# Banded attention on TensorE: query halves of 64 with their 192 keys, on quarters of the array

## The chip, the cores and the metric

The kernel runs on one core of one Trainium2 chip. The metric is the device time of one launch in microseconds, the median of three runs. All computation is in one launch; the host only lays out the inputs and outputs.

Engines are called PE (TensorE), PEld (its weight loads), DVE (VectorE), ACT (ScalarE), POOL (GpSimd) and SP (SyncE, which issues DMAs).

## The reference, cut to what matters

One step of a two-layer decoder trunk for 1024 prompt tokens and 8 sample tokens, model width 1024, fp32: a gated linear recurrence (HGRN2) layer, then a layer of sliding-window attention with 16 query heads and 2 key/value heads of 64, partial rotary, a learned sink per head, a SiLU gate, and a final RMSNorm. For a block of 128 queries the attention is

```python
tq = jnp.arange(128)[:, None]
j = jnp.arange(256)[None, :]          # keys of the block before and of the own block
rel = tq + 128 - j
mask = (rel >= 0) & (rel <= 128)
s = where(mask, q @ k.T * 64 ** -0.5, MASK_VALUE)
m = maximum(max(s), sink)
p = where(mask, exp(s - m), 0)
o = (p / (sum(p) + exp(sink - m))) @ v
```

Query t of a block sees keys t to t + 128 of its 256. So queries 0 to 63 see keys 0 to 191 and queries 64 to 127 see keys 64 to 255, which is 192 keys for either half. The first block of a sequence has no keys before it and uses the last 128 alone.

## The kernel before, in words

Everything is written by engine: each of the five engines has one function with its instructions in order, and semaphores join them. The order around the change is written out by hand.

**Weights and products.** A product of the residual stream with 128 columns of weights is a unit: 24 matmuls (8 slices of 128 features, 3 products of high and low parts in fp32r) for one of three segments of 344 tokens (`product`, L1611). Each unit accumulates in one PSUM bank, `unit_bank(u)`, and DVE reads it out. Units of the second weight matrix of the attention layer (the output projection) are in two halves of 12 matmuls, `output_product` (L1885): first half, on heads 0 to 7, within the attention steps and read out by `first_half` (L1489); second half after them (L1945). `BEFORE[u]` is the last unit that had the same bank; PE waits until that has been read. The banks are G0, G1 and G2 for the output units, and G0 and G1 for the gate units before them, because the decode part of the attention uses G2 in steps 1 to 10.

**Ahead of attention.** After the residual stream is formed, PE adds its squares (L1797), ACT makes the scale RB (L1001, L1004), and DVE waits for it (`rb1_done`, L1379) before it reads out the K/V product (`evacuate`, L1141) and rotates K (L1385 to L1389). ACT negates K into KNEG (L1015).

**The attention steps.** There are 32 query blocks q: 4 groups p of heads by 8 blocks nb of 128 queries. A block has four heads, i = 2*jj + v, where v picks partitions 0 to 63 or 64 to 127 of the query tile (the two key/value heads). The steps s = -3 to 31 run a pipeline on PE: `values(s-1)`, `turn(s)`, `scores(s+2)`, then gate products up to step 15 and 18 output products per step from step 16.

- `scores(q)` (L1831): four matmuls, one per (jj, v), with 64 feature rows, 128 queries as weights and 256 keys as moving columns (128 where nb = 0). Head v goes to bank R[v], jj to the left or right half of it. The results are negated scores.
- `minima(q)` (L1457, DVE): adds the mask, takes the minimum with the sink, writes SP_. `exponentials` (L1047, ACT), `denominators` (L1467, L1468, DVE) and `normalise` (L758, POOL) finish the probabilities.
- `turn(q)` (L1843): transposes of 128x128 into R[2] (keys before) and R[3] (own keys). ACT copies R[2] to PT[:, 0] (`copy_before`, L1057), DVE copies R[3] to PT[:, 1] (`copy_own`, L1475).
- `values(q)` (L1858): per key block and v one matmul with 128 keys as rows, 64 value columns as weights and 256 moving columns (2 heads by 128 queries), into the partitions of v in R[4].
- `gate_output(q)` (L1481, DVE): multiplies R[4] by the gate and writes it over the queries in A. `cut_slice` and `tile_hi`/`tile_lo` (L1085, L1568) split it into high and low parts for the output products.

The decode part for the 8 sample tokens lies in the same steps: scores after step 1 (L1923), values after step 9 (L1940 with 128 rows, L1941 with 8 rows, alternating), and DVE sets `d_done` in step 10.

At the very start DVE clears the five R banks (L1248).

Of the kernel before, what the change touches and what calls it, by code (L numbers as in the profile page):

```python
# [21 lines left out]
P = 128  # L22
KT = D // P
SEQ, DEC = 1024, 8
T = SEQ + DEC
NU = 3
# [3 lines left out]
NC = SEQ // P  # L30
# [12 lines left out]
N_B2 = N_BQ + HP  # L43
N_BO = N_B2 + HP - BG_FIRST
N_B3 = N_BO + KT
NBLK = N_B3 + KT
HK = KT // 2
NQ = 4 * NC
GAIN_A, GAIN_O, GAIN_KV, GAIN_B, GAIN_F = range(5)

# [36 lines left out]
def unit_bank(u):  # L88

    if u < 2 * NU:  # L90
        return u
    return u % (2 if NU * N_B2 <= u < NU * N_BO else 3)

BEFORE = [max([v for v in range(u) if unit_bank(v) == unit_bank(u)], default=-1) for u in range(NU * NBLK)]

def gates_fill(s):

    return (36, 60, 90)[s + 3] if s < 0 else min(360, 90 + 270 * (s + 1) // 16)  # L100

def output_fill(s):

    return 18 * max(0, s - 15)

GATE_END = [min(s for s in range(-3, NQ) if gates_fill(s) >= 24 * (g + 1)) for g in range(NU * (HP - BG_FIRST))]
OUT_END = [min(s for s in range(NQ) if output_fill(s) >= 12 * (g + 1)) for g in range(NU * KT)]
SLOT = (2, 3, 4, 5, 0, 1, 6, 7)  # L110
# [13 lines left out]
def half_step(h):  # L124

    if h < 6:
        return end_step(N_B2 + 2 + h // 2) + 1
    return h + 12 if h < KT else OUT_END[2 * KT + h - KT] + 1

def build(nc, ctx, ins, outs):
    fp32, fp32r, bf16, u8 = mybir.dt.float32, mybir.dt.float32r, mybir.dt.bfloat16, mybir.dt.uint8
    ALU, ACT = mybir.AluOpType, mybir.ActivationFunctionType
# [14 lines left out]
    def sb(name, shape, dt, cursor=at):  # L148
        n = size[dt]
        for s in shape[1:]:  # L150
            n *= s
        t = nc.alloc_sbuf_tensor_at(name, shape, dt, offset=cursor[0])
        cursor[0] += (n + 31) // 32 * 32
        assert cursor[0] <= nc.sbuf_top, (name, cursor[0])
        return t
# [4 lines left out]
    A = sb("A", [P, KT, T], fp32)  # L160
# [46 lines left out]
    KNEG = sb("KNEG", [P, SEQ], fp32, rb_)  # L207
    rb_[0] += 4 * SEQ
    rb_[0] += 2 * 4 * SEQ
    VP = sb("VP", [P, NC, P], fp32, [rb_[0]])  # L210
# [7 lines left out]
    PT = sb("PT", [P, 2, 512], fp32, rb_)  # L218
    rb_[0] += 2 * 4 * 4 * P
    SGR = sb("SGR", [P, 2, 2, P], fp32, rb_)  # L220
# [26 lines left out]
    G = [ctx.enter_context(nc.psum_tensor(f"G{i}", [P, 512], fp32)) for i in range(3)]  # L247
    R = [ctx.enter_context(nc.psum_tensor(f"R{i}", [P, 512], fp32)) for i in range(NBANK_R)]
    U = [*G, *R[2:5]]

    def sem(name):
        return ctx.enter_context(nc.semaphore(name))
# [91 lines left out]
    d_done = sem("d_done")  # L344
# [18 lines left out]
    pv_done = sem("pv_done")  # L363
    gated = sem("gated")
# [59 lines left out]
    def query(q):  # L424

        return divmod(q, NC)

    def key_blocks(q):
        return range(1 if q % NC == 0 else 0, 2)
# [22 lines left out]
    def pair(t, q):  # L452

        p, nb = query(q)
        return t[:, 2 * p:2 * p + 2, nb * P:(nb + 1) * P]

    def before_count(q):

        return q - q // NC
# [5 lines left out]
    def _(sp):  # L465
# [5 lines left out]
        def load_half(h):  # L471
            sp.wait_ge(*lo_value(N_B2 + 2 + h // 2 if h < 6 else N_BO + h - 6))
            ks = slice(0, HK) if h < KT else slice(HK, KT)
            sp.dma_start(raw_tile(h), w_d[N_BO + h % KT][:, ks]).then_inc(raw_half[h % 6], 16)
# [138 lines left out]
        def load_gate(q):  # L613

            if q % NC == 0:
                stored_gates(2 * (q // NC) + 1)
            if q >= 2:
                sp.wait_ge(gated, q - 1)
            sp.dma_start(SGR[:, q % 2], pair(sg_d, q)).then_inc(sg_in[q % 2], 16)
# [17 lines left out]

        for s in range(-3, NQ + 1):
            if 0 <= s + 1 < NQ:
                load_gate(s + 1)  # L640
# [3 lines left out]
            for h in range(6, 2 * KT):  # L644
                if half_step(h - 6) + 1 == s and s < NQ:
                    load_half(h)
# [14 lines left out]
        for h in range(6, 2 * KT):  # L661
            if half_step(h - 6) + 1 >= NQ:
                load_half(h)
# [464 lines left out]
    def _(dve):  # L1128
# [144 lines left out]
        for it in range(HEADS + 1):  # L1273
            r = it - 1
            for slot in range(9):
                j, i = divmod(slot, 3)
# [84 lines left out]
        def cut_stream(m):  # L1361

            dve.wait_ge(cut_hi, KT + m + 1)
            dve.wait_ge(h1_out[m % 2], 16 * (m // 2 + 1))
            dve.wait_ge(sq1_done, m + 1)
            nc.vector.tensor_tensor(XH[:, m, :], H1[:, m, :], XL[:, m, :].bitcast(fp32), ALU.subtract
                                    ).then_inc(cut_lo, 1)
# [9 lines left out]
            add_residual(m, 2)  # L1377
        cut_stream(KT - 1)
        dve.wait_ge(rb1_done, 1)  # L1379

        for i in range(NU):
            evacuate(NU * N_KV + i, i, KE)
# [43 lines left out]
        for j in range(HP):  # L1426
            prepare(N_BQ + j + 2)
            for i in range(NU):
                u = NU * (N_BQ + j) + i
# [47 lines left out]
        def gate_output(q):  # L1477

            dve.wait_ge(pv_done, q + 1)
            dve.wait_ge(sg_in[q % 2], 16 * (q // 2 + 1))  # L1480
            nc.vector.tensor_tensor(pair(A, q), R[4][:, 0:2 * P].rearrange("p (j w) -> p j w", j=2), SGR[:, q % 2],  # L1481
                                    ALU.mult).then_inc(gated, 1)

# [24 lines left out]
        for s in range(-3, NQ + 1):  # L1508
            if 0 <= s + 1 < NQ:
                denominators(s + 1)  # L1510
            if 0 <= s - 1:
                gate_output(s - 1)
# [52 lines left out]
            if 15 <= s < 18:  # L1565
                i = s - 15
# [25 lines left out]
    def _(pe):  # L1592
# [145 lines left out]
        for it in range(HEADS + 1):  # L1738
            p, r = it - 2, it - 1
# [67 lines left out]
        for i in range(2):  # L1807
            for c in range(4):
                ins = nc.tensor.transpose(R[3 + i][:, c * P:(c + 1) * P], RES[0][:, (4 * i + c) * P:(4 * i + c + 1) * P],
                                          ident[:])  # L1810
# [8 lines left out]
        def scores(q):  # L1819
            p, nb = query(q)  # L1820
            keys = slice(P if nb == 0 else 0, 2 * P)
            tok = slice((nb - 1) * P + keys.start, (nb + 1) * P)
            if q:
                pe.wait_ge(sc_read, 2 * q)
            else:
                pe.wait_ge(q_rot, HP)
                pe.wait_ge(kb_done, 1)
            for jj in range(2):
                for v in range(2):
                    rows = slice(64 * v, 64 * v + 64)  # L1830
                    ins = nc.tensor.matmul(R[v][:, 2 * P * jj + keys.start:2 * P * (jj + 1)], pair(A, q)[rows, jj],  # L1831
                                           KNEG[rows, tok], start=True, stop=True)
                ins.then_inc(sc_done, 1)

        def turn(q):
# [11 lines left out]
        def values(q):  # L1847
            p, nb = query(q)
            pe.wait_ge(pt_own, q + 1)
            if nb:  # L1850
                pe.wait_ge(pt_before, before_count(q))
            if q:
                pe.wait_ge(gated, q)
            blocks = key_blocks(q)
            for kb in blocks:
                for v in range(2):
                    rows = slice(64 * v, 64 * v + 64)
                    ins = nc.tensor.matmul(R[4][rows, 0:2 * P].rearrange("p (j w) -> p j w", j=2),  # L1858
                                           VP[:, nb - 1 + kb, rows],
                                           PT[:, kb, :].rearrange("p (j v w) -> p j v w", j=2, v=2)[:, :, v, :],  # L1860
                                           start=(kb == blocks[0]), stop=(kb == 1))
            ins.then_inc(pv_done, 1)
# [12 lines left out]
        def output_product(f, i, m, w):  # L1875

            u, h = out_unit(f, i, m), KT * f + m
            k, p = divmod(w, 3)
            if w == 0:
                pe.wait_ge(*lo_value(N_BO + h))  # L1880
                pe.wait_ge(unit_read, BEFORE[u] + 1)
            wh, wl = half_tile(WH, WXH, h), half_tile(WL, WXL, h)
            xh, xl = XL[:, HK * f + k, seg(i)], AR[:, HK * f + k, seg(i)]
            wt, x = ((wh, xh), (wh, xl), (wl, xh))[p]
            return nc.tensor.matmul(G[unit_bank(u)][:, 0:TU], wt[:, k, :], x, start=(w == 0), stop=(w == 11))  # L1885
# [12 lines left out]
        def segment_sums(i):  # L1898
            pe.wait_ge(sq2_added, (KT - 1) * (i + 1))
            nc.tensor.matmul(R[i][:, 0:TU], ones[:], SQA[:, seg(i)], start=True, stop=False)  # L1900
            pe.wait_ge(sq2_done, KT * (i + 1))
            nc.tensor.matmul(R[i][:, 0:TU], ones[:], SQ[:, (KT * i + KT - 1) % 2], start=False, stop=True
                             ).then_inc(sums2_done, 1)

        for s in range(-3, NQ):
            if s >= 1:
                values(s - 1)
# [10 lines left out]
            if s == 1:  # L1918
# [3 lines left out]
                for b in range(DEC):  # L1922
# [3 lines left out]
                                 stop=True).then_inc(d_scores, 1)  # L1926
# [8 lines left out]
            if s == 9:  # L1935
                pe.wait_ge(d_pcop, 1)
                for b in range(DEC):
# [3 lines left out]
                    ins = nc.tensor.matmul(G[2][:, cols], VN[:], PSN[:, pc], start=False, stop=True)  # L1941
# [3 lines left out]
        for i, ready in enumerate((11, 14, 16)):  # L1945
            pe.wait_ge(slice_lo, ready)
            for m in range(KT):
                for w in range(12):
                    ins = output_product(1, i, m, w)
                ins.then_inc(unit_done, 1)  # L1950
                if i and m == 1:
                    segment_sums(i - 1)
# [69 lines left out]
```

## Time and profile before

| | us |
|---|---|
| three runs | 1032.52, 1033.85, 1038.28 (median 1033.85) |
| profiled execution, its own time | 1032.45 |
| its span, first to last instruction | 1030.7 |
| mean granted TensorE clock | 0.989 |
| PE, DVE, ACT, POOL busy | 995.3, 565.1, 375.2, 427.2 |

The profile is of one execution. A group of matmuls is named by line, tiles and shape: "64*128 64x256" has 64 rows and 128 columns of weights and 256 moving columns. In the time line a row has start, length, engine, line, operation, tiles and shape, and xN says that N instructions of one line are joined; brackets at the end say how long the engine was idle before and what released it. Ends of matmuls are modelled, so lengths include the way through the array; starts are what to count with. "PEclk" is the granted clock as a share of 2.4 GHz.

### The profile page before, as it was taken

Reading aid. Unit: us, or ns where it says so; the run is one execution under the profiler, and the core shown is the slowest. Engines: PE = TensorE matmul, PEld = TensorE weight load, DVE = VectorE, ACT = ScalarE, POOL = GpSimd, SP = SyncE. Lnnn points to the kernel's source line nnn. Section 1 sums busy time; section 2 is a strip of 40 time slices with the busy share of each in tenths; the row PEclk is TensorE's granted clock in tenths of the full one; section 3 lists DMA queues with packets and bytes.
Section 4 is the critical chain, followed back from the end, with each engine's and each line's share of the span. In section 5 each row is a group of like instructions: output and inputs, shape, how many; then the busy total and the mean of one; then the engine's idle time right before and its main releaser. Section 6 shows DMA issues by size and latency. Waiting matters only on the chain.

```text
span 1030.7 us, 22050 instructions
## 1 busy us (share of the span) xinstructions
PE 995.3 (97%) x9218; PEld 927.4 (90%) x9218; DVE 565.1 (55%) x1139; ACT 375.2 (36%) x746; POOL 427.2 (41%) x302
## 2 busy tenths in 40 slices
PE   6999999999999999899999999999989999999996
PEld 6889999999999998798999999999988877778895
DVE  5254554646454554636932234357766757966634
ACT  7621313131322322424332233501026757745422
POOL 1265545363545444312244342344444434444333
PEclk9999999999999999899999999999999999999998
DMA  9411221312121213321333324211112213322103
GB/s 367 152 64 65 64 86 43 106 37 93 43 86 44 86 43 107 121 91 58 113 124 124 135 70 142 82 48 42 62 47 69 63 57 102 100 73 81 32 35 131
DMA packets 52915, 89.86 MB, mean 87 GB/s; under 512 B 15720, under 2 KB 34760, under 8 KB 52688
## 3 DMA queue, kind: packets, MB, share of 16 engines
q1 hardware_dynamic: 52816, 88.46, 26.3%
q8 instruction: 73, 1.20, 0.5%
q14 instruction: 26, 0.21, 0.1%
HBM read 70.80 MB, written 17.64 MB: 86 GB/s over the span
## 4 chain that ended last, share of the span: by engine, by line
PE 85%; DVE 4%; ACT 3%; DMA 2%; issue 2%; POOL 2%; SPq 1%; DVEq 0%; POOLq 0%; ACTq 0%
PE G L1611 54%; PE G L1885 9%; PE R L1665 3%; PE R L1831 3%; PE R L1858 3%; PE R L1843 3%; DMA ST<-xs 2%; PE R L1687 1%; PE R L1676 1%; PE R L1639 1%; PE R L1690 1%; PE R L1696 1%; DVE AR L1323 1%; DVE A L1245 1%; SPq L484 1%
## 5 line engine op out<-in xcount | busy, mean ns | idle before, releaser
L1611 PE MATMUL G<-XH,WH 128*128 128x344 f32 x1176 | 384.5, 329 | 9.5 <-ACT XH L915 7.7
L1611 PE MATMUL G<-XL,WH 128*128 128x344 f32 x1176 | 377.1, 323 | 2.9 <-DVE KE L1433 1.9
L1611 PEld LDWEIGHTS G<-XH,WH 128*128 128x128 f32 x1176 | 223.1, 190 | 17.8 <-issue 15.4
L1611 PE MATMUL G<-XH,WL 128*128 128x344 f32 x744 | 236.2, 321 | 0.0
L1611 PEld LDWEIGHTS G<-XL,WH 128*128 128x128 f32 x1176 | 222.8, 190 | 6.6 <-issue 3.2
L681 POOL TENSOR_TENSOR WL<-WR,WH 128x1024 fp32r<-128x1024 f32 x40 | 102.8, 2570 | 166.1 <-ACT WH L828 156.0
L828 ACT ACTIVATE WH<-WR 128x1024 fp32r<-128x1024 f32 x58 | 61.3, 1056 | 268.3 <-PE G L1611 160.6
L1611 PEld LDWEIGHTS G<-XH,WL 128*128 128x128 f32 x744 | 140.4, 189 | 0.0
L1611 PE MATMUL G<-XL,WL 128*128 128x344 f32 x432 | 139.5, 323 | 0.0
L712 POOL TENSOR_TENSOR K<-K,FP 128x512 f32<-128x512 f32 x48 | 76.3, 1591 | 105.7 <-PE R L1665 105.7
L758 POOL TENSOR_TENSOR SP<-SP,small 128x1024 f32<-128x1024 f32 (+1 forms) x32 | 57.2, 1787 | 108.3 <-DVE small L1468 108.3
L1611 PEld LDWEIGHTS G<-XL,WL 128*128 128x128 f32 x432 | 82.2, 190 | 0.9 <-issue 0.7
L1047 ACT ACTIVATE SP<-SP,small 128x256 f32<-128x256 f32 (+1 forms) x128 | 61.8, 484 | 46.2 <-DVE small L1457 46.2
L1611 PE MATMUL G<-GR,WH 128*128 128x344 f32 x192 | 61.5, 320 | 1.3 <-DVE KTT L1141 1.3
L1611 PE MATMUL G<-GR,WL 128*128 128x344 f32 x192 | 61.4, 320 | 0.0
L1611 PE MATMUL G<-AR,WH 128*128 128x344 f32 x192 | 61.3, 319 | 0.0
L1457 DVE CUSTOM_DVE_ANT_0 SP<-R,amask,sink 128x256 f32<-128x256 f32 (+1 forms) x128 | 52.2, 463 | 11.9 <-PE R L1831 11.5
L1885 PE MATMUL G<-XL,WH 128*128 128x344 f32 x144 | 47.9, 333 | 0.0
L774 POOL TENSOR_TENSOR KE<-KE,CS 128x1032 f32<-128x1032 f32 x8 | 27.2, 3396 | 49.5 <-DVE KE L1437 49.5
L1885 PE MATMUL G<-XL,WL 128*128 128x344 f32 x144 | 46.0, 319 | 0.0
L1885 PE MATMUL G<-AR,WH 128*128 128x344 f32 x144 | 45.9, 319 | 0.0
L1141 DVE TENSOR_TENSOR RAWQ<-G,RB 128x344 f32<-128x344 f32 x24 | 12.4, 515 | 59.9 <-PE G L1611 59.9
(261 smaller groups left out, 1739.8 us busy)
## 6 DMA issues: line engine op xcount, KB each, us to landing
WR<-w SPq DMA_DIRECT2D x58, 512.0 KB, 3.6
A<-x SPq DMA_DIRECT2D x8, 516.0 KB, 7.2
FG<-head_scales SPq DMA_DIRECT2D x8, 516.0 KB, 3.5
RESO<-x SPq DMA_DIRECT2D x8, 516.0 KB, 4.6
h_spill<-H SPq DMA_DIRECT2D x8, 516.0 KB, 3.3
gate_spill<-EV SPq DMA_DIRECT2D x24, 172.0 KB, 1.9
RES<-h_spill SPq DMA_DIRECT2D x24, 172.0 KB, 2.5
y<-H SPq DMA_DIRECT2D x24, 172.0 KB, 1.9
```

What stands on the lines that cost most here:

```text
L681: nc.gpsimd.tensor_tensor(WL[:, n % 3], WR[:, n % 3], WH[:, n % 3].bitcast(fp32), ALU.subtract).then_inc(lo_pool, 1)
L712: nc.gpsimd.tensor_tensor(low, low, decay(l, 1).unsqueeze(2).broadcast_to([P, SEQ // (2 * h), h]), ALU.mult).then_inc(upd_k, 1)
L758: nc.gpsimd.tensor_tensor(sp_, sp_, small[:, q % 2, 4, :].unsqueeze(2).broadcast_to([P, 4, keys.stop - keys.start]), ALU.mult).then_inc(p_ ...
L828: nc.scalar.activation(WH[:, n % 3], WR[:, n % 3], ACT.Copy).then_inc(hi_done, 1)
L1047: nc.scalar.activation(SP_[q % 2][:, i, keys], SP_[q % 2][:, i, keys], ACT.Exp, bias=sm[:, 0, i:i + 1], scale=-1.0, accum_out=sm[:, 2, i:i ...
L1457: ins = nc.vector.tensor_tensor_reduce(out=SP_[q % 2][:, i, keys], in0=ps[:, keys], in1=amask[:, keys], scale=1.0, scalar=sink[:, h + i:h ...
L1611: return nc.tensor.matmul(U[unit_bank(NU * n + i)][:, 0:TU], w[:, n % 3, k, :], x[:, seg(i)], start=(k == 0 and p == 0), stop=(k == KT - 1 ...
L1665: ins = nc.tensor.matmul(b[v * w:v * w + w - h, first // 2:(first + w) // 2].rearrange("p (n h) -> p n h", h=h), K[r % 2][:, first:first + ...
L1831: ins = nc.tensor.matmul(R[v][:, 2 * P * jj + keys.start:2 * P * (jj + 1)], pair(A, q)[rows, jj], KNEG[rows, tok], start=True, stop=True)
L1843: ins = nc.tensor.transpose(R[2 + kb][:, i * P:(i + 1) * P], SP_[q % 2][:, i, kb * P:(kb + 1) * P], ident[:])
L1858: ins = nc.tensor.matmul(R[4][rows, 0:2 * P].rearrange("p (j w) -> p j w", j=2), VP[:, nb - 1 + kb, rows], PT[:, kb, :].rearrange("p (j v ...
L1885: return nc.tensor.matmul(G[unit_bank(u)][:, 0:TU], wt[:, k, :], x, start=(w == 0), stop=(w == 11))
```

## The change

- `scores(q)` for nb > 0: each (jj, v) matmul becomes two, for queries 0 to 63 and 64 to 127, each with its own 192 keys: 64 rows, 64 columns of weights, 192 moving columns, eight matmuls per block. The parts of R[v] that are not written any more are cleared once: two memsets on DVE behind the wait for `rb1_done`. For nb = 0 nothing changes.
- `values(q)` for q >= 11 and nb > 0 (`two_banks`): early queries go to R[4], late ones to G[2], 128 moving columns each (2 heads by 64 queries). First, for both halves, the block of keys of which all 128 are seen (the one before for early, the own for late queries); then the 64 keys of the other block. Eight matmuls instead of four. `gate_output` then takes two instructions.
- The first-half output units use banks G0 and G1 alone; PE waits for `d_done` before values(11), and for gate_output of the last block before the third unit of the second half.

```diff
-    return u % (2 if NU * N_B2 <= u < NU * N_BO else 3)
+    return u % (2 if NU * N_B2 <= u < NU * (N_BO + KT) else 3)
...
+    def two_banks(q):
+        return q >= Q_TWO and q % NC != 0      # Q_TWO = 11
...
         dve.wait_ge(rb1_done, 1)
+        for b in R[0:2]:
+            nc.vector.memset(b[:], 0.0)
...
+            if two_banks(q):
+                for u in range(2):
+                    part = slice(64 * u, 64 * u + 64)
+                    ins = nc.vector.tensor_tensor(pair(A, q)[:, :, part], (R[4], G[2])[u][:, 0:P].rearrange(
+                        "p (j w) -> p j w", j=2), SGR[:, q % 2, :, part], ALU.mult)
+                ins.then_inc(gated, 1)
+                return
...
             for jj in range(2):
                 for v in range(2):
                     rows = slice(64 * v, 64 * v + 64)
-                    ins = nc.tensor.matmul(R[v][:, 2 * P * jj + keys.start:2 * P * (jj + 1)], pair(A, q)[rows, jj],
-                                           KNEG[rows, tok], start=True, stop=True)
+                    if nb == 0:
+                        ins = nc.tensor.matmul(R[v][:, 2 * P * jj + P:2 * P * (jj + 1)], pair(A, q)[rows, jj],
+                                               KNEG[rows, tok], start=True, stop=True)
+                        continue
+                    for u in range(0, P, 64):
+                        ins = nc.tensor.matmul(R[v][u:u + 64, 2 * P * jj + u:2 * P * jj + u + 192],
+                                               pair(A, q)[rows, jj, u:u + 64],
+                                               KNEG[rows, tok.start + u:tok.start + u + 192], start=True, stop=True)
                 ins.then_inc(sc_done, 1)
...
+            if two_banks(q):
+                if q == Q_TWO:
+                    pe.wait_ge(d_done, 1)
+                for near in range(2):
+                    for u in range(2):
+                        kb = u ^ near
+                        ks = slice(64 * kb ^ 64, (64 * kb ^ 64) + 64) if near else slice(0, P)
+                        for v in range(2):
+                            rows = slice(64 * v, 64 * v + 64)
+                            ins = nc.tensor.matmul(
+                                (R[4], G[2])[u][rows, 0:P].rearrange("p (j w) -> p j w", j=2),
+                                VP[ks, nb - 1 + kb, rows],
+                                PT[ks, kb, :].rearrange("p (j v w) -> p j v w", j=2, v=2)[:, :, v, 64 * u:64 * u + 64],
+                                start=not near, stop=bool(near))
+                ins.then_inc(pv_done, 1)
+                return
...
             for m in range(KT):
+                if i == 0 and m == 2:
+                    pe.wait_ge(gated, NQ)
```

## Rows read from the trace of the kernel before

**Rows 1.** The page: PE's busy time, and shares of the chain that ended last.
```profile
PE 995.3 (97%) x9218; PEld 927.4 (90%) x9218; DVE 565.1 (55%) x1139; ACT 375.2 (36%) x746; POOL 427.2 (41%) x302
...
PE 85%; DVE 4%; ACT 3%; DMA 2%; issue 2%; POOL 2%; SPq 1%; DVEq 0%; POOLq 0%; ACTq 0%
```

**Rows 2.** Busy us by stretch: length, PE, PEld, DVE, ACT, POOL, clock, DMA share, GB/s.
```profile
764.80:976.00 211.20, 211.19 (x1429) 171.01 (x1430) 148.94 (x514) 130.80 (x418) 86.39 (x66) 0.98 0.25 74
888.60:960.90 72.30, 72.30 (x498) 57.28 (x498) 52.02 (x189) 40.55 (x144) 32.06 (x27) 1.00 0.33 92
```

**Rows 3.** Time line of PE: start us, length us, operation (one step and its predecessor's values).
```profile
888.63 1.08 PE L1858 MATMUL R<-PT,VP 128*64 128x256 f32 x8
...
894.75 1.08 PE L1858 MATMUL R<-PT,VP 128*64 128x256 f32 x8
895.76 1.09 PE L1843 MATMUL R<-ident,SP 128*128 128x128 f32 x8
896.78 1.13 PE L1831 MATMUL R<-KNEG,A 64*128 64x256 f32 x8
897.85 0.42 PE L1885 MATMUL G<-XL,WH 128*128 128x344 f32 x1
```

**Rows 4.** Time line of PE: scores of a first block, 128 keys.
```profile
867.74 0.71 PE L1831 MATMUL R<-KNEG,A 64*128 64x128 f32 x8
```

**Rows 5.** Values: records (min/median/max ns), and the time line with one key block.
```profile
L1858 PE MATMUL R<-PT,VP x240: 379/379/689, 781.2 to 971.3; 128*64 128x256 f32 x120
...
882.95 0.65 PE L1858 MATMUL R<-PT,VP 128*64 128x256 f32 x4
```

**Rows 6.** Time line of PE: decode scores, then decode values of 128 and 8 rows.
```profile
786.63 1.85 PE L1923 MATMUL G<-QS,RES 128*128 128x16 f32 x16
...
835.41 0.39 PE L1941 MATMUL G<-PSN,VN 8*128 8x16 f32 x2
835.73 0.40 PE L1940 MATMUL G<-PST,RES 128*128 128x16 f32 x2
836.06 0.39 PE L1941 MATMUL G<-PSN,VN 8*128 8x16 f32 x2
```

**Rows 7.** Time lines of DVE and PE: K/V evacuation, PE's next unit, five memsets.
```profile
614.60 1.36 DVE L1141 TENSOR_TENSOR KE<-G,RB 128x344 f32<-128x344 f32 x3 [4.75 <-ACT RB L1004]
...
615.27 0.40 PE L1611 MATMUL G<-XL,WH 128*128 128x344 f32 x1 [0.43 <-DVE KE L1141]
...
0.92 2.65 DVE L1248 MEMSET R<- 128x512 f32 x5 [0.92 <-PEq L2012]
```

**Rows 8.** Time lines of DVE and PE where an evacuation is closest to its bank's reuse.
```profile
969.66 0.50 DVE L1489 TENSOR_TENSOR H<-G,RES 128x344 f32<-128x344 f32 x1
...
971.64 0.43 PE L1885 MATMUL G<-XL,WH 128*128 128x344 f32 x1
```

**Rows 9.** Durations of two DVE lines, ns min/median/max.
```profile
L1481 DVE TENSOR_TENSOR A<-R,SGR x32: 407/410/426, 782.9 to 971.8; 128x256 f32<-128x256 f32 x32
...
L1489 DVE TENSOR_TENSOR H<-G,RES x24: 500/515/517, 884.6 to 970.7; 128x344 f32<-128x344 f32 x24
```

**Rows 10.** Busy us from step 15 to 17; columns as in rows 2.
```profile
877.00:894.70 17.70, 17.70 (x121) 13.82 (x119) 17.10 (x48) 13.94 (x41) 8.62 (x7) 1.00 0.34 99
```

**Rows 11.** Time lines of DVE, POOL and PE in step 17 and after.
```profile
887.12 0.68 DVE L1475 COPY PT<-R 128x512 f32<-128x512 f32 x1
...
886.96 1.89 POOL L758 TENSOR_TENSOR SP<-SP,small 128x1024 f32<-128x1024 f32 x1 [3.94 <-DVE small L1468]
...
889.64 1.09 PE L1843 MATMUL R<-ident,SP 128*128 128x128 f32 x8
```

**Rows 12.** Busy us and granted clock around its falls; columns as in rows 2.
```profile
672.90:676.31 3.41, 1.47 (x10) 1.22 (x9) 2.88 (x7) 0.36 (x1) 0.00 (x0) 1.00 0.21 24
676.31:679.73 3.42, 3.42 (x14) 3.42 (x13) 2.24 (x2) 0.00 (x0) 2.27 (x1) 0.50 0.32 129
...
765.06:768.47 3.41, 3.41 (x17) 3.19 (x16) 3.28 (x14) 1.65 (x4) 0.00 (x0) 0.50 0.24 78
...
840.15:843.57 3.42, 3.42 (x17) 2.25 (x17) 0.42 (x1) 0.24 (x1) 0.00 (x0) 0.50 0.00 0
```

More of the change, by code:

```diff
@@ L48 @@
 NQ = 4 * NC
+Q_TWO = 11
 GAIN_A, GAIN_O, GAIN_KV, GAIN_B, GAIN_F = range(5)
```

## The prediction

> **What bounds the kernel now.** I read the page's busy shares and its chain of waits first. PE is busy 97% of the span, and 85% of the chain that ended last is PE's own work [rows 1], so what PE no longer does comes off the end, unless another engine takes over. The edit lies in the attention stage. The table of stretches says that from the first scores (764.8) to the last values (976.0) PE has a record open for 211.19 of 211.20 us, while DVE is busy for 148.94; in the steady steps from 888.6 to 960.9 it is PE 72.30 and DVE 52.02, or 72% [rows 2]. PE's order there is fixed by hand: values(s-1), turn(s), scores(s+2), then a share of the gate or output products.
>
> PE's records overlap, so their sum tells nothing; the time line tells when each group starts. A step whose predecessor's values start at 888.63 reads values 894.75, transposes 895.76, scores 896.78, first output product 897.85 [rows 3]: 1.01, 1.02 and 1.07 us, of 6.12 from values to values. 
> **Scores, per query block with nb > 0 (28 of 32).** The edit halves each matmul by queries and gives each half the 192 keys it can see: eight matmuls on 64x64 quarters, still four rounds if all four quarters of a round run at once. What 64 columns fewer are worth can be read off, since the first blocks already have 128 keys: that group takes 0.71 us against 1.13 [rows 3, 4], 0.42 over four rounds, 0.105 for 128 columns in a round. 192 columns lie halfway: -0.21. The weights of a quarter have 64 columns and not 128; the first load of a group is not hidden. The values, with 64 weight columns and the same 256 moving ones, take 1.08 where the scores take 1.13 [rows 3]: -0.05. I take off 0.01 for four starts per round in place of two. Sum -0.25 per block, **28 x 0.25 = -7.0 us**. The bounds are -0.26 and, if nothing overlaps beyond the pairs of now, a loss (rival 3).
>
> **Values, from query block 11, nb > 0 (19 blocks: 11 to 15, 17 to 23, 25 to 31).** Now: four rounds of 256 columns. The group of one key block has two rounds and takes 0.65 [rows 5], that of two takes 1.08, so a round is 0.216. A round of 128 columns is 0.216 - 0.105 = 0.11. The new form has the near keys over all 128 rows, early queries then late ones, v side by side: four rounds of 0.11. The far keys are 64 rows each and need four quarters: two rounds of 0.11. Six rounds are 0.66 in place of 0.86: -0.20. But between the two parts the array goes from 128x64 to 64x64 tiles. What such a change costs the decode part shows: sixteen records with 16 columns take 1.85 us without one, 0.106 each. L1940 and L1941 alternate between 128 and 8 rows, and four of their records take 0.65 (835.41 to 836.06) [rows 6]. That is 0.43 plus 0.22 for two changes, 0.11 each. Their loads are in the 0.106 already; mine was hidden and now is not. A first load of 64 columns costs 0.65 - 0.38 (the last record) - 0.216 = 0.05. So -0.20 + 0.16 = -0.04 per block, **19 x 0.04 = -0.8 us**. Ends: -3.8 if the change of tiles costs nothing, +1 if it costs double here. I take the alternating row, the only one where the row grouping alone changes.
>
> **The two memsets.** They stand behind the wait for rb1_done and ahead of the first evacuation of the K/V product. DVE begins this at 614.60, and PE starts its next unit only at 615.27, released by it [rows 7]: PE waits for exactly what is now delayed. Queued behind them on DVE are the K and V evacuations, the rotation, and through it ACT's KNEG copy; those have until the scores at 764.8. Five such memsets take 2.65 us [rows 7], two 1.06. None of it is covered: **+1.06 us**, at least 0.9, as memsets of now follow one another.
>
> **Two banks for the first-half output products.** G2 now belongs to the values, so unit t waits for the evacuation of t-2, not t-3. The tightest of the 24 places: the unit that starts at 971.64 needs the evacuation at 969.66, until 970.16, 1.5 us before [rows 8]. A step gets 0.3 us shorter, so it costs nothing. What hides it is DVE's lead of 1.5 us; without it each late evacuation stops PE one for one. Wait for d_done at block 11: DVE does that after step 10's values, PE asks in step 12; nothing. Wait for gated = 32 ahead of the third unit of the last phase: two units later, about 4 us after the gate; nothing.
>
> **gate_output in two halves.** 256 columns take 0.41 us, 344 take 0.515 [rows 9]: 1.2 ns a column and 0.10 fixed. Two of 128 are 0.5: +0.10 to 0.15 per block on DVE. Behind it in DVE's queue stand copy_own, on which the next values wait, and the minima. In the steady steps DVE has 1.7 us to spare. In steps 15 to 18 it has not: from 877.0 to 894.7 it is busy 17.1 of 17.7 us [rows 10]. copy_own ends at 887.80 for values at 888.63, 0.83 ahead; POOL's normalise ends at 888.85 for transposes at 889.64, 0.79 ahead [rows 3, 11]. Over these three steps PE gains 0.85 and DVE loses 0.3, so the margin of 0.8 is used up, and some of the gain goes: **+0.3 us** (0 to 1).
>
> **Sum.** -7.0 - 0.8 + 1.06 + 0.3 = -6.4 us. The profiled execution took 1032.45 (span 1030.7), which gives 1026.0. It is the low end of what is shown; the three runs are 1032.52, 1033.85 and 1038.28. The middle of all four is 1033.2, so I forecast **1026.8**.
>
> **The clock.** Of the granted clock the stretches show three falls to 0.50 (1.2 GHz) near this work, each 3.4 us long: at 676.31 after PE was busy 1.47 of 3.41 us, at 765.06 as the first scores begin, and at 840.15 behind the decode part with its 16-column matmuls [rows 12]. Half a clock for 3.4 us costs 1.7 us. The edit moves all of this against whatever ticks there, so one fall may go or come: 1.7 either way in the range.
>
> **Rivals.**
> 1. The change of tiles inside the values is free. For: rows and columns of the tiles nest. Against: rows 6. A further 19 x 0.16 = 3.0 us: 1023.8. Chance 0.07.
> 2. The longer stop ahead of 615.27 makes the clock fall. PE idled there for 0.43 us and the clock stayed [rows 7]; with 1.06 more it comes nearer to the stretch before 676.31, where PE was idle for 1.94 [rows 12]. +1.7: 1028.5. Chance 0.12.
> 3. **Slower.** Row halves and column halves don't combine: of four quarters only two run at once. The place is each scores group and the far part of the values. Eight rounds of 0.163 (0.216 less 64 columns) in place of four of 0.216 are +0.44, less 0.05 for the load: +0.39 x 28 = +10.9. The values get two more rounds, 0.22 - 0.04 = +0.18 x 19 = +3.4. With the memsets and DVE's part 1033.2 + 15.7 = 1048.9. It decides as soon as a scores group takes over 1.13. For it: no row here shows a 64x64 tile. Against: both kinds of halves overlap fully on their own. This is also how it would look if the change didn't do what it says. Chance 0.06.
> 4. Loads don't hide behind a matmul of the same rows. Each round of scores is then 0.163 + 0.05 = 0.213 against 0.216, and only the first load is saved: -0.06 x 28 = -1.7. In the values each of six rounds is 0.16, 0.96 + 0.16 against 0.86: +0.26 x 19 = +4.9. 1033.2 + 4.6 = 1037.8. Against: the values of now load 64 columns per round over all rows, and their round is 0.216, just the 256 columns [rows 5]. Chance 0.06. The Trainium skill has it as a rule (TensorE: Matmul & The Clock Gate, the part on packing small matmuls): a weight load overlaps running matmuls "only when row_grp differs". Two quarters side by side have the same rows. The trace of before disagrees in the values' column halves.
> 5. DVE, or the normalise behind it, paces steps 15 to 31. Then only the scores of blocks 1 to 15 pay, 14 x 0.25 = 3.5: 1033.2 - 3.5 + 1.06 = 1030.8. For: rows 10, 11. Against: 72% in the later steps [rows 2]. Chance 0.09.
>
> **How the numbers follow.** The forecast has 0.60, from 1024.5 to 1029.5 with one fall of the clock either way; the rivals have 0.40. A measurement of this kernel can tell about 0.5%, 5.2 us, from no change, so faster means under 1028.7. The forecast lies under it 9 times in 10 (0.54), rival 1 always (0.07), rival 2 half (0.06): 0.67. Rivals 3 and 4, lower by what noise may hide of the latter, give slower 0.08. The rest is 0.25. The range leaves out rivals 3 and 4 and a little at the low end: 1022.8 to 1033.0.
>
> **What would show it.** Scores groups with 16 records take 0.87 to 0.90 us, from 1.13. The values of block 17 and later take about 1.04, with a gap of 0.16 ahead of the far part; 0.88 would be rival 1. PE's stop ahead of 615.27 grows by 1.06. Steady steps shrink from 6.12 to about 5.83. Some idle time of PE on copy_own or normalise shows near blocks 17 and 18. Scores groups above 1.1 us would prove the main term wrong; a PE that waits for L1489 would prove wrong that two banks are enough.

## The result, and the profile after

The changed kernel takes 1027.74 us, the median of six runs (1026.95 to 1028.80). Six runs of the kernel before have a median of 1036.01 (1032.52 to 1038.28). The ratio is 0.9929, with a 95% interval of 0.9908 to 0.9951: 0.5 to 0.9% faster, 7.4 us in the middle. All ratios are of executions in the chip's usual state; two of the kernel before, of 1216 and 2476 us, fell out of it and are left out of those of e1 to e4. The profiled execution took 1026.95 with a span of 1025.2, against 1032.45 and 1030.7. The forecast was 1026.8, within 1022.8 to 1033.0.

The time line of PE after the change has, in block 18, the values in four shapes, then the transposes, the scores and the first output product (columns as in rows 3):

```profile
886.63 0.44 PE L1884 MATMUL R<-PT,VP 128*64 128x128 f32 x4
...
892.45 0.44 PE L1884 MATMUL R<-PT,VP 128*64 128x128 f32 x4
892.72 0.39 PE L1884 MATMUL G<-PT,VP 128*64 128x128 f32 x4
893.04 0.33 PE L1884 MATMUL R<-PT,VP 64*64 64x128 f32 x2
893.05 0.33 PE L1884 MATMUL G<-PT,VP 64*64 64x128 f32 x2
893.20 0.28 PE L1884 MATMUL R<-PT,VP 64*64 64x128 f32 x2
893.21 0.28 PE L1884 MATMUL G<-PT,VP 64*64 64x128 f32 x2
893.42 1.09 PE L1863 MATMUL R<-ident,SP 128*128 128x128 f32 x8
894.44 0.88 PE L1850 MATMUL R<-KNEG,A 64*64 64x192 f32 x16
895.25 0.42 PE L1921 MATMUL G<-XL,WH 128*128 128x344 f32 x1
```

Against [rows 3]: from the start of the scores to the next product 0.81 us instead of 1.07, sixteen records in place of eight. From the values to the transposes 0.97 instead of 1.01. The transposes are as before, 1.02. The step takes 5.82 instead of 6.12. Within the values, the early queries' near part starts at 892.45, the late ones' at 892.72, the far part at 893.04. From 892.72 to 893.04 is 0.32, of which two rounds fill 0.22: 0.10 is the gap that the change of tiles leaves. The first round of the far part takes 0.16 (893.04 to 893.20), where its 128 columns fill 0.11: the 0.05 more is the load that nothing hides.

DVE and PE at the memsets, which answer to [rows 7]:

```profile
616.11 1.03 DVE L1386 MEMSET R<- 128x512 f32 x2 [4.90 <-ACT RB L1009]
617.04 1.34 DVE L1146 TENSOR_TENSOR KE<-G,RB 128x344 f32<-128x344 f32 x3
...
617.69 0.40 PE L1625 MATMUL G<-XL,WH 128*128 128x344 f32 x1 [1.50 <-DVE KE L1146]
```

PE is idle for 1.50 us there instead of 0.43: 1.07 more. The busy table of the steady steps and of steps 15 to 17 (as rows 2 and 10, shifted), and DVE, POOL and PE around block 17 (as rows 11):

```profile
886.60:955.60 69.00, 69.00 (x673) 56.89 (x672) 52.99 (x201) 41.06 (x144) 32.43 (x27) 1.00 0.36 98
875.50:892.45 16.95, 16.71 (x159) 13.53 (x158) 16.57 (x48) 13.38 (x40) 7.98 (x6) 1.00 0.32 92
...
885.50 0.68 DVE L1482 COPY PT<-R 128x512 f32<-128x512 f32 x1
...
885.33 1.89 POOL L763 TENSOR_TENSOR SP<-SP,small 128x1024 f32<-128x1024 f32 x1 [4.05 <-DVE small L1475]
...
878.19 0.43 PE L1921 MATMUL G<-XL,WH 128*128 128x344 f32 x1 [0.24 <-DVE AR L1582]
```

DVE is at 77% of the steady steps, from 72%. At block 17 copy_own ends at 886.18 for values at 886.63, so 0.45 us is left of 0.83; normalise ends at 887.22 for the transposes of block 18 at 887.60, 0.38 left of 0.79. PE waits for neither. It does wait once, 0.24 us, at the first output product, in step 16, for the splitting of the first output tile (L1582).

**Where the time went.** The table compares one stretch in all executions, from the first values to those of the last block. In e8, e9 and e11 the transposes stand ahead of the values; there it begins with the transposes of block 1, so that every row has the same work in it. The granted clock falls at other moments in each execution. In the changed kernel a record of the gate products follows the last one after 0.287 us at 0.50 (ten from 767.58 to 770.45) and after 0.157 at 1.00 (twenty from 774.29 to 777.44). So "corrected" is the stretch less half of the time that it spent at 0.50, and the last column compares that.

| kernel | stretch | of it at 0.50 | corrected | to before |
|---|---|---|---|---|
| before | 189.45 | 3.4 | 187.7 | |
| changed | 182.30 | 3.4 | 180.6 | -7.1 |
| e1 scores only | 184.59 | 6.8 | 181.2 | -6.6 |
| e2 values only | 188.65 | 3.4 | 186.9 | -0.8 |
| e3 memsets only | 190.82 | 6.8 | 187.4 | -0.3 |
| e4 two banks only | 190.81 | 6.8 | 187.4 | -0.3 |
| e5 changed, no memsets | 183.80 | 6.8 | 180.4 | -7.4 |
| e6 changed, far part 128 rows | 184.75 | 6.8 | 181.3 | -6.4 |
| e7 changed, 256 keys | 190.56 | 10.2 | 185.4 | -2.3 |
| e8 changed, transposes first | 179.43 | 6.8 | 176.0 | -11.7 |
| e9 before, transposes first | 188.03 | 6.8 | 184.6 | -3.1 |
| e10 changed, decode sorted | 180.92 | 3.4 | 179.2 | -8.5 |
| e11 together | 176.62 | 6.8 | 173.2 | -14.5 |

The correction is good to some 0.3 us. e3 and e4 do the same work there as the kernel before; with 3.4 us more at 0.50 they take 1.36 us more, and not 1.7. So half is a little too much: against the kernel before, rows with 6.8 stand about 0.3 too low, and e7's 0.6. Two of the 28 shortened scores groups lie ahead of the stretch.

Outside the stretch the profiled execution lost 1.36 us before the memsets. Two stops of PE grew by more than that together, and the rest came back elsewhere: the stop near 411, in which ACT waits for the DMA of the head scales, took 6.0 us instead of 5.2, and 0.8 was another wait in the recurrence, at L1679. The edit touches neither. 1.07 went to the memsets. A fall of the clock at 676.3 didn't happen, the one at 765 was twice as long.

### The profile page after: what moved, and what is told of

The parts are those of the page before. It is cut to its first block, busy times and chain, and to the rows that moved or that the text cites. A ratio compares the mean times of both kernels' runs of the same rounds, so it can differ in the third digit from the quotient of the medians.

```text
span 1025.2 us, 22823 instructions
## 1 busy us (share of the span) xinstructions
PE 987.0 (96%) x9594; PEld 924.8 (90%) x9594; DVE 569.3 (56%) x1160; ACT 375.3 (37%) x746; POOL 428.3 (42%) x302
## 4 chain that ended last, share of the span: by engine, by line
PE 83%; DVE 5%; DMA 3%; ACT 3%; issue 2%; POOL 2%; SPq 1%; DVEq 0%; POOLq 0%; ACTq 0%
PE G L1625 53%; PE G L1921 9%; PE R L1679 3%; PE R L1863 3%; PE R L1850 2%; DMA ST<-xs 2%; PE R L1701 1%; PE R L1690 1%; PE R L1653 1%; PE R L1884 1%; PE R L1704 1%; DMA FG<-head_scales 1%; PE R L1894 1%; PE R L1710 1%; DVE AR L1328 1%
```

## The experiments

All ratios are to the kernel before, run on the same chip, with their 95% interval.

**e1, scores alone.** The change with `two_banks` never true, three banks, no wait for gated.

```diff
-Q_TWO = 11
+Q_TWO = 99
-    return u % (2 if NU * N_B2 <= u < NU * (N_BO + KT) else 3)
+    return u % (2 if NU * N_B2 <= u < NU * N_BO else 3)
```

> Scores on quarters with the memsets, values and banks as before. Theory (PE sets the pace of the attention steps, each part pays by itself): groups of 16 score records take 0.88 us and the start of the next operation comes 0.81 us after theirs instead of 1.07, in 28 blocks, -7.0 us; the memsets add 1.07; together -5.9 us against the kernel before. Rival (the values' change or the two banks give a larger part than 0.9 us, as the medians of the whole change differ by 8.3 us and its parts sum to 6.8): less than -4.5 us here.

Measured 0.9957 (0.9944 to 0.9970), 1028.40 us: -4.5 us, -3.1 to -5.8, where -5.9 was expected and -4.5 drew the line. So the total alone doesn't decide. The trace does:

```profile
899.83 1.08 PE L1894 MATMUL R<-PT,VP 128*64 128x256 f32 x8
900.85 1.09 PE L1863 MATMUL R<-ident,SP 128*128 128x128 f32 x8
901.87 0.88 PE L1850 MATMUL R<-KNEG,A 64*64 64x192 f32 x16
...
902.68 0.42 PE L1921 MATMUL G<-XL,WXH 128*128 128x344 f32 x1
```

Scores to product 0.81. The stretch has 26 of the 28 blocks, 26 x 0.253 = 6.6, less 0.2 for a wait at L1582 (below). It got 6.6 shorter, or 6.3 by what was said of the correction. -5.9 lies just outside the interval of the ratio, and the clocks of the runs on record account for it. Time lost to the clock, taken as (1 - granted clock) x span and averaged, is 13.4 us in e1's six executions and 12.0 in those of the kernel before (the clocks are on record to 0.001, which is 1 us of a span). With that taken off, the means are 1015.1 and 1021.9, 6.7 apart.

**e2, values alone.** The changed kernel with the scores of before and no memsets.

> Values on two banks from block 11, scores and memsets as before. Theory: the transposes start 0.968 us after the values instead of 1.015, in 19 blocks: -0.9 us, inside what the runs scatter. Rival (the two-bank form pays more, by earlier copies or gate multiplications): over 2 us faster. Rival (the second DVE instruction or the two banks make PE wait): no gain or a loss, with idle time of PE ahead of the output products or values.

Measured 0.9997 (0.9984 to 1.0010), and 0.97 us from values (900.74) to transposes (901.71):

```profile
900.74 0.44 PE L1876 MATMUL R<-PT,VP 128*64 128x128 f32 x4
...
901.33 0.33 PE L1876 MATMUL R<-PT,VP 64*64 64x128 f32 x2
...
901.71 0.55 PE L1855 MATMUL R<-ident,SP 128*128 128x128 f32 x3
```

The stretch is 0.8 us shorter (18 of the 19 blocks by 0.047 are 0.85). A gain over 2 us is excluded; nothing waits for the second instruction of DVE. This half of the edit pays less than a measurement can tell.

**e3, memsets alone.**

```diff
         dve.wait_ge(rb1_done, 1)
+        for b in R[0:2]:
+            nc.vector.memset(b[:], 0.0)
```

> The kernel before with the two memsets alone. Theory: PE's idle time ahead of the first unit after the K/V product grows from 0.43 to 1.50 us and all later work shifts by 1.07. Rival (the longer stop brings a fall of the clock there): a stretch at 0.50 that begins near 616 us and 1.7 us more, +2.8. Rival (later waits take the shift up): PE's stop of 1.9 us before the queries' second group shrinks by as much, 0.

Measured 1.0025 (1.0006 to 1.0043), +2.6 us in the middle. In the trace PE idles 1.49 us at this point and the clock stays at 1.00 around it:

```profile
616.58 1.03 DVE L1381 MEMSET R<- 128x512 f32 x2 [4.90 <-ACT RB L1004]
...
618.16 0.39 PE L1613 MATMUL G<-XL,WH 128*128 128x344 f32 x1 [1.49 <-DVE KE L1141]
```

From the sums of squares (611.94) to this unit are 6.22 us, before 5.16 (610.11 to 615.27). PE's later stop of 1.9 us is still 1.9. So the price is 1.07 and nothing takes it up. The rest of the +2.6 is inside the interval, and e3's eight executions lost 14.2 us to the clock where those of the kernel before lost 12.0. With this taken off the two means are equal (1021.8 and 1021.9), so the totals neither show the 1.07 nor exclude it, and need nothing beyond it. In no trace with the longer stop (the changed kernel, e1, e3, e6, e7, e8, e10) does the clock fall near it.

**e4, two banks alone.**

```diff
-    return u % (2 if NU * N_B2 <= u < NU * N_BO else 3)
+    return u % (2 if NU * N_B2 <= u < NU * (N_BO + KT) else 3)
```

> The kernel before with two banks instead of three for the first-half output products. Theory: the evacuations lead by at least 1.5 us, 0. Rival (evacuations arrive late in steps 15 to 18, where DVE is full): idle time of PE on L1489, up to 1 us.

Measured 1.0007 (0.9985 to 1.0028), with no idle time of PE on L1489. Two banks cost nothing.

**e5, the changed kernel without the memsets.** It computes the same.

> The changed kernel without the two memsets (R0 and R1 keep finite results of earlier stages where the scores no longer write, and the mask's 1e30 covers them). Theory: PE's stop ahead of the first unit after the K/V product is 0.43 us again instead of 1.50, all later work comes 1.07 us earlier, ratio about 1 us below the changed kernel's, 0.992. Rival (something later takes it up): same as the changed kernel.

Measured 0.9942 (0.9928 to 0.9956), where 0.992 was expected. PE's idle time ahead of that unit is 0.43 again:

```profile
617.33 0.40 PE L1623 MATMUL G<-XL,WH 128*128 128x344 f32 x1 [0.43 <-DVE KE L1146]
```

The 1.07 us is back in the trace, but the totals don't show it: e5's median (1028.39) is not below the changed kernel's. The intervals of the two overlap, and 1 us is too little for them. With the time lost to the clock taken off, the means are 1013.9 and 1014.7, which points the same way as the trace.

**e6, the far part with 128 rows.** The 64 further keys have probability 0.

```diff
-                        ks = slice(64 * kb ^ 64, (64 * kb ^ 64) + 64) if near else slice(0, P)
+                        ks = slice(0, P)
```

> The changed kernel, but the far keys of the values go as 128 rows too (the extra 64 have probability 0), so the tiles stay 128x64 within the values. Theory (a change of tiles costs 0.10 us and an exposed load of 0.05): the far part has four rounds of 0.11 instead of two, +0.22, and loses the change, -0.15: transposes start about 1.03 us after the values instead of 0.968, +0.06 in 19 blocks, +1.2 us. Rival (the gap of 0.16 ahead of the far part is something else, such as a switch to the other bank): transposes 1.19 us after the values, +4 us.

```profile
893.45 0.44 PE L1884 MATMUL R<-PT,VP 128*64 128x128 f32 x4
893.72 0.39 PE L1884 MATMUL G<-PT,VP 128*64 128x128 f32 x4
893.94 0.39 PE L1884 MATMUL R<-PT,VP 128*64 128x128 f32 x4
894.16 0.39 PE L1884 MATMUL G<-PT,VP 128*64 128x128 f32 x4
894.48 1.09 PE L1863 MATMUL R<-ident,SP 128*128 128x128 f32 x8
```

Values to transposes 1.03, as expected, and the far part starts 0.22 after the last near one, without a gap. It has the same two banks in turn, so the 0.15 of the changed kernel (0.10 of gap, 0.05 of load) belongs to the change of tiles and not to the bank. Ratio 0.9952 (0.9938 to 0.9966). The quarters win 0.06 us per block only, because they pay for the change.

**e7, quarters with all 256 keys.**

```diff
-                        ins = nc.tensor.matmul(R[v][u:u + 64, 2 * P * jj + u:2 * P * jj + u + 192],
+                        ins = nc.tensor.matmul(R[v][u:u + 64, 2 * P * jj:2 * P * (jj + 1)],
...
-                                               KNEG[rows, tok.start + u:tok.start + u + 192], start=True, stop=True)
+                                               KNEG[rows, tok], start=True, stop=True)
```

> The changed kernel with all 256 keys for both query halves: 64x64 quarters, 256 moving columns. Theory (the keys left out are the gain, the quarters only let them be left out): four rounds of 0.216 us, next operation 1.03 us after the scores' start, against 0.81 with 192 keys and 1.07 with halves: +0.22 in 28 blocks, +6 us against the changed kernel, so about -1 against before. Rival (the shorter loads or the finer tiles are much of the gain): clearly below 1.03.

```profile
898.54 1.09 PE L1850 MATMUL R<-KNEG,A 64*64 64x256 f32 x16
899.56 0.42 PE L1921 MATMUL G<-XL,WH 128*128 128x344 f32 x1
```

Scores to product 1.02, ratio 0.9998 (0.9985 to 1.0011). Quarters alone give 0.04 of the 0.25 us. The 64 keys left out give 0.21.

**e8, transposes ahead of the values.**

```diff
-            if s >= 1:
-                values(s - 1)
             if s >= 0:
                 turn(s)
+            if s >= 1:
+                values(s - 1)
```

> The changed kernel with another order in each step: transposes ahead of the values, so that products and transposes (both 128x128) stand next to each other, and from block 11 the values' far part (64x64) next to the scores (64x64). Theory (each change of tiles costs about 0.15 us of PE wherever it stands): one change less in 31 steps and a second less in 19, 50 x 0.15 = 7.5 us faster than the changed kernel, ratio to before about 0.985. Rival (the gaps belong to the semaphore waits at the head of each group): no gain. Rival (normalise on POOL had only 0.8 us to spare in steps 15 to 18 and now is needed 1 us earlier): part of the gain comes back as idle time of PE on POOL, 1 to 3 us.

```profile
893.26 1.04 PE L1863 MATMUL R<-ident,SP 128*128 128x128 f32 x8
894.22 0.44 PE L1884 MATMUL R<-PT,VP 128*64 128x128 f32 x4
...
894.98 0.28 PE L1884 MATMUL G<-PT,VP 64*64 64x128 f32 x2
895.08 0.83 PE L1850 MATMUL R<-KNEG,A 64*64 64x192 f32 x16
...
898.76 1.03 PE L1863 MATMUL R<-ident,SP 128*128 128x128 f32 x8
```

The step is 5.50 us, from 5.82. The transposes take 0.96 from start to start (1.02 before), the values 0.86 (0.97), and the scores follow the far part 0.10 after its last round started, without a gap. Ratio 0.9898 (0.9878 to 0.9918), and a median 4.0 us under the changed kernel's. The stretch is 4.6 us shorter than the changed kernel's, where 7.5 were expected.

The 7.5 counted too many places. Steps 30 and 31 have no scores, so the order takes away no change there: 29 steps and not 31. And the far part has scores on quarters behind it in 14 of the 19 blocks. Blocks 29 to 31 have none behind them, and 13 and 21 have those of a first block, on 64x128 tiles, behind a gap of 0.10; values to scores is still 0.97 there:

```profile
865.38 0.44 PE L1884 MATMUL R<-PT,VP 128*64 128x128 f32 x4
...
866.13 0.28 PE L1884 MATMUL R<-PT,VP 64*64 64x128 f32 x2
...
866.35 0.71 PE L1846 MATMUL R<-KNEG,A 64*128 64x128 f32 x8
```

43 places by 0.15 are 6.5 us, and 1.7 of them PE idles, which leaves 4.8. The idle time is 1.40 in front of the transposes of block 18, for normalise, and 0.55 instead of 0.24 for L1582:

```profile
877.91 0.43 PE L1921 MATMUL G<-XL,WH 128*128 128x344 f32 x1 [0.55 <-DVE AR L1582]
...
887.69 1.09 PE L1863 MATMUL R<-ident,SP 128*128 128x128 f32 x8 [1.40 <-POOL SP L763]
```

The semaphore waits at the head of each group are as before, so the gaps did not belong to them. The price of a change and the rival on POOL are right, the number of changes was not.

**e9, the same order on the kernel before.**

> The kernel before (halves, 256 keys) with the transposes ahead of the values. Theory (a change of tiles costs 0.15 us each): one change less in 31 steps, since products and transposes stand together and the other changes stay: -4.6 us, less about 1 us that comes back as idle time of PE on POOL near block 17, ratio about 0.9965. Rival (the gain of the same order on the changed kernel came from elsewhere): 1.0.

Measured 0.9976 (0.9958 to 0.9994). The stretch is 3.1 us shorter. There are 29 places here too: 29 x 0.15, less 0.74 us of idle time on POOL and 0.16 ahead of the first output product, would be 3.5. With the time lost to the clock taken off, the means of the executions are 3.0 apart (1018.1 and 1021.1).

```profile
890.18 1.09 PE L1843 MATMUL R<-ident,SP 128*128 128x128 f32 x8 [0.74 <-POOL SP L758]
```

**e10, decode values sorted by tile.** The changed kernel; only the order of the sixteen matmuls and the flags that open and close the accumulation differ.

```diff
-                for b in range(DEC):
+                for new in range(2):
+                    for b in range(DEC):
...
```

> The changed kernel with the decode part's values sorted by tile: the eight matmuls with 128 rows, then the eight with 8 rows. Theory (a change of tiles costs 0.11 us there): the part takes 32 x 0.106 + 0.2 = 3.6 us instead of 5.1, 1.5 us less, and a fall of the clock behind it may get shorter or go. Rival (8-row matmuls are slow by themselves): 5.1 us still.

```profile
L1980 PE MATMUL G<-PST,RES x16: 178/263/263, 833.5 to 835.1; 128*128 128x16 f32 x16
...
L1978 PE MATMUL G<-PSN,VN x16: 257/258/278, 835.3 to 837.0; 8*128 8x16 f32 x16
```

Both halves take 1.7 us from the first to the last start, about 0.11 a record, and the next values start at 837.18: 3.7 us instead of 5.1. The 8-row matmuls are no slower than the others. Ratio 0.9903 (0.9882 to 0.9924); the stretch is 1.4 us shorter than the changed kernel's.

**e11, together.** e5, e8 and e10, and tiles 1 and 2 split in steps 18 and 20:

```diff
-            if 15 <= s < 18:
-                i = s - 15
+            if s in (15, 18, 20):
+                i = (15, 18, 20).index(s)
```

> What paid, together: the changed kernel without memsets, transposes ahead of the values, decode values sorted by tile, and the splitting of output tiles 1 and 2 (ACT L1085, DVE L1568 of the kernel before) in steps 18 and 20 instead of 16 and 17, since PE needs them in steps 21 and 26. Theory: against the changed kernel -1.1 (memsets), -7.5 (50 changes of tiles), -1.5 (decode), and PE's idle 1.4 us on POOL in step 17 gone: 10 us faster than the changed kernel, ratio to before about 0.983. Rival (DVE is short of time in later steps too): idle time of PE on POOL or DVE moves to steps 18 to 21.

Measured 0.9848 (0.9822 to 0.9874), median 1019.09 us. It beats both kernels: 15.7 us under the kernel before, 8 to 9 under the changed one. 10 under the changed one were expected, with 50 changes in the count. The stretch is 7.4 us shorter than the changed kernel's (43 x 0.15 + 1.4 = 7.9, less 0.3 more on L1580), and the 1.07 of the memsets lies ahead of it. PE waits for POOL no more; 0.55 us for the first output tile is what stays.

Not tried: the values wholly on quarters, which would save the change of tiles within them. Each output needs keys from both row halves, and the two halves would add into one bank at the same time. What that does no run here shows.

## Why the prediction was right, point by point

- **Scores.** -0.25 per block from 28 blocks: measured 1.064 to 0.811, -0.253 (rows above, e1). The halfway between the 128-key and 256-key groups held, as did the shorter first load: e7 separates them as 0.21 and 0.04.
- **Values.** -0.04 per block: -0.047. The price of a change of tiles, taken from the decode part, was 0.11 + 0.05; the gap is 0.10 and the load 0.05. e6, e8, e9 and e10 agree: without the change within the values its 0.15 is gone (e6), and each change taken out elsewhere gives back 0.15 (e8, e9), or 0.10 where the load is in the pace of the records already (e10).
- **Memsets.** +1.06: +1.07 (e3, e5). Nothing later took it up.
- **Two banks, the two waits.** 0: no idle time (e4).
- **DVE's part.** Forecast +0.3, measured +0.24, and that they agree is luck: it is another wait, with another cause. I put it at block 17, on copy_own or normalise, and found the margin of 0.8 used up. It was used to half, 0.38 to 0.45 us are left. PE waited two steps earlier, at the first output product, for L1582, which I had not looked at. Before, that splitting ended 0.06 us ahead of the product (rows of DVE and PE before; then of DVE after):

```profile
878.28 1.58 DVE L1568 TENSOR_TENSOR AR<-A,XL 128x1376 fp32r<-128x1376 f32 x1
...
879.92 0.43 PE L1885 MATMUL G<-XL,WH 128*128 128x344 f32 x1
...
880.07 0.41 DVE L1481 TENSOR_TENSOR A<-R,SGR 128x256 f32<-128x256 f32 x1
880.39 0.68 DVE L1475 COPY PT<-R 128x512 f32<-128x512 f32 x1
```

```profile
878.34 0.28 DVE L1491 TENSOR_TENSOR A<-R,SGR 128x128 f32<-128x128 f32 x1
878.54 0.28 DVE L1491 TENSOR_TENSOR A<-G,SGR 128x128 f32<-128x128 f32 x1
878.73 0.68 DVE L1482 COPY PT<-R 128x512 f32<-128x512 f32 x1
```

What DVE does there starts from a gate unit that PE has just finished; between that unit and the product PE has values(15) and scores(18), which became 0.04 and 0.25 us shorter. 0.29 less the margin of 0.06 is the wait. The second gate instruction has no part in it: e1 has only one, its values are as before, and it waits 0.19, which is 0.25 less 0.06:

```profile
879.64 0.43 PE L1921 MATMUL G<-XL,WH 128*128 128x344 f32 x1 [0.19 <-DVE AR L1582]
```

Nor does the second instruction cost DVE what I gave. From gate_output to the next instruction are 0.39 us with two and 0.32 with one, +0.07 in place of 0.10 to 0.15: the records overlap, so their lengths (two of 0.28 for 0.41) say too much. e8 does meet the shortage at block 18, as the transposes come earlier.
- **Sum.** -6.4 forecast. By the measured terms: -0.253 x 28 - 0.047 x 19 + 1.07 + 0.24 = -6.7. The ratio gives -7.4 with -5.1 to -9.5. That 1027.74 lies only 0.9 us from 1026.8 is in part luck: the forecast took its -6.4 off 1033.2, the middle of the four times then known, and the six executions in the comparison have a median of 1036.0. The parts above are the test.
- **The clock.** One fall went and one became longer, as the range allowed.
- **Rivals.** 1 is refuted by the gap. 2 by seven traces. 3 by the group of 0.88 us, where it had over 1.1: all four quarters run at once. 4 by the same group: four rounds and 0.15 at the change make the 0.81, so a round is 0.16, where rival 4 had 0.21, and the loads hide. So in this kernel a load does overlap matmuls on the same rows, against the sentence quoted from the Trainium skill (TensorE: Matmul & The Clock Gate, packing small matmuls). 5 is refuted by the steady steps of 5.82 us, with DVE at 77%; e8 shows how near it was in steps 16 to 18.

## What to carry to other kernels

Count what PE does between starts, not the lengths of records, and price a finer tiling by rounds: a round costs its moving columns, with two tiles in it or four (0.216 us for 256 columns in both, e7). Each change of the tiles' shape cost 0.15 us here (0.20 ahead of the old scores, with 128 weight columns: their 1.064 less four rounds of 0.216), so neighbours in PE's order should have the same shape. Count the places from PE's order step by step: 43 changes went in e8, not the 50 that were counted by blocks. Sorting gave 4.6 us on top of the change, where the quarters by themselves gave 28 x 0.04 and the packing of the values almost nothing; the bulk of the change, 28 x 0.21 us, is the keys left out. Before PE is made faster, look at every place where it is released just in time: the one that took some of the gain had 0.06 us to spare and was not among those examined. Anything put ahead of an evacuation that PE already waits for is paid in full, even 1 us of memset.

## What the runs showed that was not expected

**The clock's falls differ between executions and move the time more than any part of the edit but the scores.** The kernel before and e4 do the same work on PE in the same order. Their spans are 1030.7 and 1036.1, their mean clocks 0.989 and 0.984. (1 - 0.989) x 1030.7 is 11.3 us of lost clock, (1 - 0.984) x 1036.1 is 16.6: of the 5.4 us between them this would be 5.2. By the 1.36 us that 3.4 more at 0.50 cost in e3 and e4, it is some 4. The same stretch of both, the kernel before first:

```profile
835.00:850.00 15.00, 15.00 (x94) 11.97 (x94) 5.91 (x24) 5.82 (x22) 3.69 (x4) 0.89 0.19 65
```

```profile
835.00:850.00 15.00, 15.00 (x84) 12.60 (x84) 6.24 (x22) 5.59 (x19) 4.86 (x4) 0.77 0.21 65
```

Over the thirteen traces of this case the places are few: after the stop near 411 and at the end in all, behind the decode part in all, at the first scores (765) in all but e7's, near 676 in seven, near 33 in five. What differs is whether the clock falls and for how long: 3.4, 6.8 or once 10.2 us at the first scores and behind the decode part. So executions of one kernel spread over 6 us (the kernel before, above) to 9 (e4's twelve, 1028.71 to 1037.99), and a part worth 1 us, such as the memsets, can be read from a trace but hardly from medians.
